# Hybrid mixer with expert retrieval on one core: another number of row steps for each stage of a front, an earlier first dot product, and a shorter pooling

## The chip, the cores and the metric

The kernel runs on one core of a Trainium2 chip. The metric is device time in microseconds (us). A difference of less than 0.3% (12 us) cannot be told from no change.

## The reference

One decoder layer over 1024 tokens of width 1024, in float32, batch 1, depth 1. Cut to what matters:

```python
proj = h @ w_in                       # pool values | z | x,B,C | dt | two gates
a    = pool_mixer(pool_in)            # 4 groups, trailing means of 2/4/8/16 tokens minus the token itself, per-group 256x256 map
m    = ssm_mixer(z, xbc, dt_raw)      # depthwise conv of 4 taps, SiLU, chunked scan (chunk 128), gate, grouped RMSNorm, @ ssm_out
h    = layer_norm(alpha * h + (sigmoid(g_pool) * a + sigmoid(g_ssm) * m) @ w_out)
# expert retrieval, 8 heads:
q = h @ w_q                           # per head two halves of 128
s = q . sub_keys                      # 128 scores per half; top 16 of each, 16 best sums of pairs -> 16 experts, softmax -> gate
hdot = sum_d h[t, d] * expert_u[idx[t, k], d]
out  = sum_k gelu(hdot[t, k]) * gate[t, k] * expert_v[idx[t, k], :]
h    = layer_norm(alpha * h + out)
```

Each token chooses 8 x 16 = 128 experts. For each it needs one row of 4 KB of `expert_u` and one of `expert_v`.

## The kernel before

**Two streams of work.** The tokens are cut into four superchunks of 256 (two tiles of 128). The *front* of a superchunk computes all that comes before the expert rows: projections, pooling, convolution, scan, merge, first layer norm, queries, top-k. The *rows* part gathers expert rows and uses them. A *pair* is one (tile, head, k): 128 tokens, one gather of 128 rows of `eu` for a dot product and one gather of 128 rows of `ev` for a weighted sum. There are 8 tiles x 128 = 1024 pairs.

**Steps.** Time is written by hand in steps: step p has the dot product of pair p on DVE (`dot`, L1401), and the weighted row of the pair 28 steps earlier (`LEAD`). That row is summed by DVE (`sum_row`, L1426) or by PE, as a matmul with a diagonal matrix (L549; 4 matmul records for a row), which ACT builds from the weights (L851, `vdiag`). The front of superchunk c is woven between the pairs of superchunk c-1: `until(p)` issues the pairs up to step p, `weave(p, front, n)` does so and lets n pieces of the front's DVE work in between, evenly spread. PE and ACT have programs of their own with the same step numbers, and meet DVE only at semaphores. ACT's GELU of a group of 16 pairs waits for its 16 dots, the weights of the group come two steps before its first row is due, and everything behind such a wait on ACT waits too.

**Stages of a front** (steps before: `STEPS` = 256 in all):

- A, four times (j = 0 to 3), 32 steps each: eight weight blocks of 1 MB on PE (L471, L479), pooling on DVE, convolution, transposes, then from offset 19 on the scan, in which PE, ACT and DVE take turns. DVE's pooling (`pooling`, L1144 to L1165) must end before PE's pool matmul (L580). From offset 20 DVE weaves the scan over the last 12 steps.
- Pair, four times 7 steps: gates and the output map of the scan. W, 16 steps: `w_out` and the layer norm.
- D0 and D1, 42 steps each: queries and scores on PE for four heads, then top-k, candidates and the choice of 16 experts on DVE (L1313 to L1383). D0 makes the indices of heads 0 to 3, D1 those of heads 4 to 7, in both tiles.

`EARLY` = 24: 24 dots come before superchunk 1's front, inside D1 of superchunk 0. The first front has no pairs beside it until then, and its last front ends at step 24 + 3 x 256 = 792. After step 800 (`PAIRED`) nothing is left but pairs, and u and v rows come in one gather of 8 KB rows (`euv`, L447); this stretch is called the tail.

**Who sums a row.** `share_of_pe(p)` gives PE a share of the rows due at step p; `assign_rows` adds the shares up and gives PE a row each time they reach 1, but never the first four and last three of a tile.

```python
    if off < ATC:
        return 0.4 if off % PA >= 19 else 0.0
    if off < ATW:
        return 0.0
    if off < ATD:
        return 0.4
    return 0.75
```

**Buffers and queues.** Single rows go through 12 buffers of 512 KB (`ROWS`), used in turn in the fixed order `ORDER`. POOL issues each gather (L432) once the pair of 12 places before has been used, and it waits for the indices of a half (`idx_ready`) only at that half's first dot. SP loads the weight blocks into a ring of four, each when PE has used its place. All these transfers share the core's 16 DMA engines.

Of the kernel before, what the change touches and what calls it, by code (L numbers as in the profile page):

```python
# [18 lines left out]
NC = SEQ // T  # L19
# [24 lines left out]
MAINS = AJ * MA + MC + MW + MD  # L44
TA, TW, TD = 12, 4, 8
TURNS = AJ * TA + TW + TD
# [8 lines left out]
EARLY = 24  # L55
STEPS = UNITS * TOPK
PAIRS = NC * STEPS
TILE = PH * TOPK
PA, PC, PW, PD = 32, 7, 16, 42
ATC = AJ * PA  # L60
ATW = ATC + 4 * PC
ATD = ATW + PW

# [7 lines left out]

def share_of_pe(p):
# [49 lines left out]
def build(nc, x, xt, wblocks, wdt, poolw, pscale, convw, convb, dtb, alog, dskip, normw,  # L122
          ln1g, ln1b, ln2g, ln2b, subkt, eu, ev, euv, out):
    with ExitStack() as ctx:
# [33 lines left out]
        pcoef = sb("pcoef", [P, 4, 4])  # L158
# [119 lines left out]
        DECAYS = (7, 8, 10, 11)  # L278
        TURNED = 10
        CONV = (0, 1, 3, 4)  # L280
# [22 lines left out]

        def turns(c, m):


            if c > 0:
                return c * TURNS - AJ * len(CONV) + m
            j = min(m // TA, AJ)
            return m - j * len(CONV) - (sum(n < m - j * TA for n in CONV) if j < AJ else 0)  # L310

        def emptied(eng, c, m):

            eng.wait_ge(main_free, c * MAINS + m + BANKS)

# [4 lines left out]
        def step(c, off):  # L320

            return EARLY + (c - 1) * STEPS + off

# [25 lines left out]
        def _(sp):  # L349
# [17 lines left out]
            def load_xt(c):  # L367
                sp.dma_start(xT[:, :, :], xt[:, :, ds(c * T, T)]).then_inc(xt_ready, 16)

            def superchunk(c):  # L370
# [12 lines left out]
                sp.dma_start(xres, x[ds(c * T, T), :].rearrange("(t p) d -> p t d", p=P)).then_inc(xres_ready, 16)  # L383
# [21 lines left out]
        def _(pool):  # L405
# [18 lines left out]
            for n, (table, q, _, _) in enumerate(ORDER):  # L424
                c, u, k = q // STEPS, q // TOPK % UNITS, q % TOPK
# [9 lines left out]
            for n, (q, _, _) in enumerate(BOTH):  # L435
                c, u, k = q // STEPS, q // TOPK % UNITS, q % TOPK
# [16 lines left out]
        def _(pe):  # L453
# [5 lines left out]
            def bank(c, m, n):  # L459
                pe.wait_ge(main_free, c * MAINS + m + n + 1)  # L460
                return main[n % 2]

            def turn_bank(c, m, n):
                pe.wait_ge(turn_free, turns(c, m + n) + 1)
                return turn[n % 2]

            def channels(dst_, w, src):

                for ct in range(2):
                    for k in range(KD):  # L470
                        last = pe.matmul(dst_[:, ct * T:(ct + 1) * T], w[:, k, ct * P:(ct + 1) * P], src[:, k, :],  # L471
# [3 lines left out]
            def tokens(dst_, w, src):  # L475

                for t in range(NT):
# [615 lines left out]
        def _(dve):  # L1093
# [180 lines left out]
            def front_w(c):  # L1274

                for t in range(NT):
# [24 lines left out]
                    if t == 1:  # L1301
                        dve.drain()
# [331 lines left out]
```

## Time and profile before

| | |
|---|---|
| median of 3 runs | 3923.23 us (3921.2 to 3933.7) |
| the profiled execution: its own time | 3919.56 us |
| the profiled execution: span of its instructions | 3917.5 us |
| busy: PE, DVE, ACT, POOL | 79%, 78%, 24%, 54% |
| bytes moved | 1334 MB, 340 GB/s in the mean |

The span is the time from the first to the last instruction; the own time is 2.1 us longer. Busy times are unions of an engine's instructions. A DMA share of 1.00 says that each of the 16 engines had a packet under way all the time, not that it moved the most bytes it can, so the rate beside it is to be read too. The granted clock is that of PE as a share of 2.4 GHz, and its lower level is 0.50 (1.2 GHz).

### The profile page before, as it was taken

The page shows a single profiled execution, that of the slowest core. Times are in us where ns is not written, and L with a number is a line of the kernel's source. Part 1 is how long each engine was busy: PE and PEld are TensorE (multiplying, and loading weights), DVE is VectorE, ACT ScalarE, POOL GpSimd, SP SyncE. Part 2 cuts the span into 40 slices and gives each one's busy share as a digit, 9 for nine tenths or more (in the row PEclk, how much of TensorE's full clock was granted, in tenths as well). Part 3 has the DMA queues.
Part 4 walks back from the last instruction along what each step waited for, and adds up shares of the span by engine and source line. Part 5 has one row for each costly group of instructions (what it writes and reads, how often), then busy time and mean ns, then how long its engine had stood idle before and what let it go on. Part 6 is the DMA issues. An engine that isn't in the chain of part 4 may idle for free. (4 is left out here: it accounts for less than half of the span.)

```text
span 3917.5 us, 39965 instructions
## 1 busy us (share of the span) xinstructions
PE 3098.7 (79%) x12052; PEld 2225.5 (57%) x12052; DVE 3043.0 (78%) x8003; ACT 923.6 (24%) x2201; POOL 2108.0 (54%) x1839
## 2 busy tenths in 40 slices
PE   8999963899987777999898767998887766565665
PEld 7888852677776445777676435776775432121221
DVE  4442289878887899888877999888877898677667
ACT  3332102244412112344312112343311111011101
POOL 0000014667766667676665677766665667555553
PEclk9999986899998898999998888999998887786877
DMA  4333347999999999999999999999999999999997
GB/s 160 108 113 126 143 155 250 337 375 395 399 397 402 326 376 366 383 394 399 399 380 397 346 366 375 377 395 368 385 375 397 328 335 356 422 422 421 422 422 327
DMA packets 306565, 1333.72 MB, mean 340 GB/s; under 512 B 34352, under 2 KB 38832, under 8 KB 249008
## 3 DMA queue, kind: packets, MB, share of 16 engines
q0 software_dynamic: 262656, 1073.86, 71.0%
q1 hardware_dynamic: 42400, 252.61, 16.4%
q10 hardware_dynamic: 1296, 4.72, 0.3%
q8 instruction: 97, 1.59, 0.2%
q14 instruction: 116, 0.95, 0.1%
HBM read 1326.85 MB, written 4.19 MB: 340 GB/s over the span
## 5 line engine op out<-in xcount | busy, mean ns | idle before, releaser
L432 POOL DMA_INDIRECT rowbuf<-eu,idx x800 | 902.2, 1128 | 1002.0 <-DVE idx L1382 535.9
L1401 DVE CUSTOM_DVE_ANT_0 rowbuf<-rowbuf,hb 128x1024 f32<-128x1024 f32 x884 | 1078.0, 1220 | 155.2 <-DMA rowbuf<-eu,idx 79.9
L432 POOL DMA_INDIRECT rowbuf<-ev,idx x800 | 918.6, 1148 | 485.6 <-PE vbank L549 231.6
L549 PE MATMUL vbank<-rowbuf,vdiag 128*128 128x512 f32 x1340 | 750.4, 703 | 354.5 <-ACT vdiag L851 237.9
L471 PE MATMUL main<-xT,ring 128*128 128x256 f32 x3584 | 795.8, 382 | 79.1 <-ACT mm L894 67.2
L471 PEld LDWEIGHTS main<-xT,ring 128*128 128x128 f32 x3584 | 688.5, 192 | 182.5 <-issue 87.9
L1426 DVE SCALAR_TENSOR_TENSOR acc<-rowbuf,hact,acc 128x1024 f32<-128x1024 f32 x549 | 705.1, 1284 | 101.9 <-DMA rowbuf<-ev,idx 93.7
L549 PEld LDWEIGHTS vbank<-rowbuf,vdiag 128*128 128x128 f32 x1340 | 281.4, 223 | 742.3 <-issue 409.6
L851 ACT ACTIVATE vdiag<-ident,hact 128x128 f32<-128x128 f32 x417 | 149.1, 393 | 468.1 <-DVE hact L1409 463.6
L654 PE MATMUL main<-late,ring 128*128 128x256 f32 x1024 | 233.0, 390 | 21.1 <-issue 15.3
L471 PE MATMUL main<-early,ring 128*128 128x256 f32 x1024 | 232.6, 387 | 0.7 <-ACT early L1014 0.7
L654 PEld LDWEIGHTS main<-late,ring 128*128 128x128 f32 x1024 | 199.4, 196 | 53.8 <-issue 18.7
L479 PE MATMUL main<-ring,xT 128*128 128x256 f32 x1024 | 226.2, 379 | 0.0
L471 PEld LDWEIGHTS main<-early,ring 128*128 128x128 f32 x1024 | 199.4, 195 | 40.8 <-issue 12.9
L479 PEld LDWEIGHTS main<-ring,xT 128*128 128x128 f32 x1024 | 194.5, 190 | 26.5
L1368 DVE SCALAR_TENSOR_TENSOR late<-iota,late,merged 128x50 f32<-128x50 f32 x1024 | 206.9, 266 | 0.8
L534 PE MATMUL turn<-craw_ln,cdiag 128*128 128x256 f32 x768 | 173.8, 378 | 0.0
L447 POOL DMA_INDIRECT rowbuf<-euv,idx x84 | 108.1, 1287 | 95.1 <-DVE acc L1426 77.6
L534 PEld LDWEIGHTS turn<-craw_ln,cdiag 128*128 128x128 f32 x768 | 145.3, 189 | 20.6
L669 PE MATMUL main<-ring,merged 128*128 128x256 f32 x512 | 119.0, 395 | 20.8 <-DVE merged L1271 20.8
L549 PE MATMUL vbank<-ring,vdiag 128*128 128x512 f32 x128 | 83.2, 797 | 60.1 <-ACT vdiag L851 60.1
L669 PEld LDWEIGHTS main<-ring,merged 128*128 128x128 f32 x512 | 101.5, 199 | 40.2 <-DVE merged L1271 22.4
(227 smaller groups left out, 3433.1 us busy)
## 6 DMA issues: line engine op xcount, KB each, us to landing
ring<-wblocks SPq DMA_DIRECT2D x224, 1024.0 KB, 8.1
rowbuf<-eu,idx POOLq DMA_INDIRECT x800, 8.5
rowbuf<-ev,idx POOLq DMA_INDIRECT x800, 8.4
xT<-xt SPq DMA_DIRECT2D x4, 1024.0 KB, 17.1
pw<-poolw SPq DMA_DIRECT2D x16, 256.0 KB, 8.2
zy<-x SPq DMA_DIRECT2D x4, 1024.0 KB, 12.7
h_out<-acc ACTq DMA_DIRECT2D x8, 512.0 KB, 7.8
craw_ln<-ln1g SPq DMA_DIRECT2D x4, 512.0 KB, 15.2
```

The source lines that it names most:

```text
L432: pool.indirect_dma_start(rows[r], None, (eu, ev)[table], bass.IndirectOffsetOnAxis(ap=idx[c % 2][:, u, k:k + 1], axis=0)).then_inc(row_re ...
L447: pool.indirect_dma_start(both[r], None, euv, bass.IndirectOffsetOnAxis(ap=idx[c % 2][:, u, k:k + 1], axis=0)).then_inc(both_ready[r], 16)
L471: last = pe.matmul(dst_[:, ct * T:(ct + 1) * T], w[:, k, ct * P:(ct + 1) * P], src[:, k, :], start=(k == 0), stop=(k == KD - 1))
L479: last = pe.matmul(dst_[:, t * 256:(t + 1) * 256], src[:, k, t * P:(t + 1) * P], w[:, k, :], start=(k == 0), stop=(k == KD - 1))
L534: last = pe.matmul(dst_[:, ct * T:(ct + 1) * T], cdiag[:, ct, k, :], craw[:, n % 2, ct, k:k + T], start=(k == 0), stop=(k == TAPS - 1))
L549: last = pe.matmul(vbank[half][:, :], vdiag[:, n % DIAGS, :], r[:, half * 512:(half + 1) * 512], start=first, stop=False, skip_group_check ...
L654: last = pe.matmul(dst_[:, ct * T:(ct + 1) * T], (lo, hi)[k // KD][:, k % KD, ct * P:(ct + 1) * P], yT[:, k, :], start=(k == 0), stop=(k = ...
L669: last = pe.matmul(dst_[:, n * 256:(n + 1) * 256], merged[:, k, t * P:(t + 1) * P], w[:, k, :], start=(k == 0), stop=(k == KD - 1))
L851: act.activation(vdiag[:, n % DIAGS, :], ident[:, :], ACT.Copy, scale=hact[:, g % 2, q % TOPK:q % TOPK + 1]).then_inc(vdiag_ready, 1)
L1368: dve.scalar_tensor_tensor(out=sel1[:, k, :], in0=iota[:, :], scalar=posf[:, u, k:k + 1], in1=candi[:, u, :], op0=ALU.is_equal, op1=ALU.mu ...
L1401: last = dve.tensor_tensor_reduce(r, r, hb[c % 2][:, t, :], 1.0, 0.0, ALU.mult, ALU.add, hdot[:, g % 2, k:k + 1])
L1426: dve.scalar_tensor_tensor(out=a, in0=r, scalar=hact[:, g % 2, k:k + 1], in1=a, op0=ALU.mult, op1=ALU.add).then_inc(row_free, 1)
```

## The change

- **Steps by stage.** `WIDTHS` gives the steps of A, pair, W, D0 and D1: 128, 28, 16, 42, 30 for superchunk 0 and 112, 28, 16, 52, 48 for the others (before: 128, 28, 16, 42, 42 for all). A front of a later superchunk still has 256 steps. All places within a stage are scaled to its new length and rounded down: `place(c, x)` gives a function from the old offset to the step. One j of A now has 28 steps, and its old offset 19 lies at 16, old 20 at 17, old 30 at 26.
- **First dots.** `EARLY` is 30: dot products begin with the first step of D1 of superchunk 0, where before 18 of its 42 steps went by first. The last front ends at step 798.
- **Shares.** PE's shares of rows are a table: 0.4 in the scan part of A, 0.4 in W, 0.75 up to step offset 30 of D (old offsets) and 1.0 after it, for superchunks 1 to 3. In the tail 0.6 as before.
- **Pooling.** Group j needs one window only. DVE now makes j+1 doublings instead of four, and one combining operation at the end instead of one after each (two for superchunk 0). The table of coefficients `pcoef` goes.
- **Bookkeeping.** Sizes, bank numbers and semaphore counts come from a list of tiles by superchunk (`CHUNK`), which is 2, 2, 2, 2, so that the numbers are the old ones. `scan_post` gets one more wait.

```diff
+CHUNK = (2, 2, 2, 2)
+NC = len(CHUNK)
-EARLY = 24
-STEPS = UNITS * TOPK
+WIDTHS = ((128, 28, 16, 42, 30),) + ((112, 28, 16, 52, 48),) * 3
+EARLY = 30
+BEGIN = [EARLY + sum(map(sum, WIDTHS[1:c])) - (0 if c else sum(WIDTHS[0])) for c in range(NC)]
+END = EARLY + sum(map(sum, WIDTHS[1:]))
+EDGES = (0, ATC, ATW, ATD, ATD + PD, ATD + 2 * PD)
+
+def step(c, off):
+    stage = max(n for n in range(5) if EDGES[n] <= max(off, 0))
+    length = EDGES[stage + 1] - EDGES[stage]
+    return BEGIN[c] + sum(WIDTHS[c][:stage]) + (off - EDGES[stage]) * WIDTHS[c][stage] // length
...
 def share_of_pe(p):
-    at, off = divmod(p - EARLY, STEPS)
-    if at == NC - 1:
+    if p >= END:
         return 0.6
+    c, off = position(p)
     if off < ATC:
-        return 0.4 if off % PA >= 19 else 0.0
+        return SHARES[c][0] if off % PA >= 19 else 0.0
     if off < ATW:
         return 0.0
     if off < ATD:
-        return 0.4
-    return 0.75
+        return SHARES[c][1]
+    return SHARES[c][2] if off < ATD + 30 else SHARES[c][3]
+
+SHARES = ((0.0, 0.0, 0.0, 1.0),) + ((0.4, 0.4, 0.75, 1.0),) * 3
...
+        def place(c, x):
+            return lambda off: step(c, x + off)
...
             def pooling(c, j, first):
                 dve.wait_ge(pool_raw, c * AJ + j + 1)
-                E = HALO + T
+                tc = CHUNK[c] * P
+                E = HALO + tc
                 src, dst_, reach = praw, psa, 1
-                for w in range(4):
+                for w in range(j + 1):
                     lo = 2 * reach - 1
                     dve.tensor_tensor(dst_[:, :, lo:E], src[:, :, lo:E], src[:, :, lo - reach:E - reach], ALU.add)
                     dve.drain()
...
+                    if w < j:
+                        src, dst_, reach = dst_, (psb if dst_ is psa else psa), 2 * reach
+                        yield
...
+                dve.scalar_tensor_tensor(out=pooled[:, :, start:tc], in0=dst_[:, :, HALO + start:E], scalar=1.0 / WINDOWS[j],
+                                         in1=praw[:, :, HALO + start:E], op0=ALU.mult, op1=ALU.subtract
+                                         ).then_inc(pool_done, 1)
...
                 y = yg[:, t, gg * GW:(gg + 1) * GW]
+                if s == 1:
+                    emptied(dve, c, j * MA + 10)
                 dve.tensor_tensor(y, yt1[:, :], zs[:, t, gg * GW:(gg + 1) * GW], ALU.mult)
...
             for c in range(NC):
                 for j in range(AJ):
-                    o = step(c, j * PA)
-                    until(o + 4)
+                    o = place(c, j * PA)
+                    until(o(4))
...
-                        weave(o + 12, pooling(c, j, False), 4)
-                    until(o + 16)
-                    weave(o + 18, merge_pool(c, j), 1)
-                    until(o + 20)
-                    weave(o + 32, scan(c, j), 18)
+                        weave(o(12), pooling(c, j, False), 4)
+                    until(o(16))
+                    weave(o(18), merge_pool(c, j), 1)
+                    until(o(20))
+                    weave(o(32), scan(c, j), 8 * CHUNK[c] + 2)
...
-                until(o + 5)
-                weave(o + PD, front_d(c, 0), 40)
-                weave(o + 2 * PD, front_d(c, 1), 40)
+                until(o(5))
+                weave(o(PD), front_d(c, 0), 18 * CHUNK[c] + 4)
+                weave(o(2 * PD), front_d(c, 1), 18 * CHUNK[c] + 4)
```

## Rows read from the trace of the kernel before

**Rows 1.** Page: span, busy times, and the DMA share in 40 equal slices.

```profile
span 3917.5 us, 39965 instructions
...
PE 3098.7 (79%) x12052; PEld 2225.5 (57%) x12052; DVE 3043.0 (78%) x8003; ACT 923.6 (24%) x2201; POOL 2108.0 (54%) x1839
...
DMA  4333347999999999999999999999999999999997
```

**Rows 2.** Stretches: length, busy PE, PEld, DVE, ACT, POOL, clock, DMA share, GB/s.

```profile
557.00:653.00 96.00, 28.80 (x126) 24.80 (x125) 88.53 (x530) 12.07 (x28) 33.80 (x35) 0.64 0.66 223
653.00:1087.00 434.00, 379.75 (x1732) 308.55 (x1730) 376.04 (x614) 160.92 (x394) 300.62 (x252) 0.93 0.97 374
1525.00:1957.00 432.00, 394.92 (x1814) 322.62 (x1813) 385.73 (x626) 171.08 (x418) 302.84 (x258) 0.96 1.00 394
1957.00:2120.00 163.00, 136.16 (x591) 111.75 (x592) 122.78 (x169) 25.04 (x44) 99.32 (x87) 0.91 0.98 389
2120.00:2269.00 149.00, 126.02 (x427) 79.76 (x426) 127.66 (x593) 27.98 (x63) 94.93 (x86) 0.89 0.96 363
2269.00:2399.00 130.00, 85.53 (x193) 39.86 (x192) 122.33 (x577) 14.29 (x39) 92.53 (x83) 0.84 0.96 352
2399.00:2842.00 443.00, 396.97 (x1814) 323.43 (x1813) 385.35 (x626) 170.87 (x417) 300.28 (x257) 0.95 0.98 383
2724.00:2842.00 118.00, 101.90 (x464) 83.11 (x464) 95.44 (x155) 43.32 (x106) 74.09 (x64) 0.92 0.93 356
3284.00:3899.00 615.00, 365.47 (x574) 128.94 (x575) 431.73 (x651) 65.73 (x206) 320.44 (x258) 0.77 1.00 415
```

**Rows 3.** L1401 alone (dots, two records each): DVE busy, clock, DMA share, rate.

```profile
557.00:653.00 96.00, 28.45 (x47) 0.64 0.66 223
557.00:683.00 126.00, 43.08 (x71) 0.67 0.74 255
1525.00:1957.00 432.00, 157.90 (x257) 0.96 1.00 394
2120.00:2399.00 279.00, 102.41 (x167) 0.87 0.96 358
```

**Rows 4.** L1426 alone (rows summed on DVE): the same columns.

```profile
1525.00:1957.00 432.00, 137.57 (x107) 0.96 1.00 394
2120.00:2399.00 279.00, 27.90 (x22) 0.87 0.96 358
```

**Rows 5.** L549 alone (rows on PE, four records each): PE, PEld, clock, DMA.

```profile
1525.00:1957.00 432.00, 42.12 (x80) 15.38 (x80) 0.96 1.00 394
2120.00:2269.00 149.00, 70.04 (x132) 27.19 (x132) 0.89 0.96 363
2269.00:2399.00 130.00, 73.21 (x124) 28.21 (x124) 0.84 0.96 352
```

**Rows 6.** All engines in short stretches of D and of one j.

```profile
2244.00:2268.00 24.00, 23.02 (x96) 16.55 (x95) 23.55 (x139) 3.92 (x9) 17.00 (x16) 1.00 1.02 409
2304.00:2328.00 24.00, 14.19 (x25) 5.41 (x24) 21.99 (x91) 3.95 (x10) 17.34 (x14) 0.86 0.91 316
1641.00:1699.00 58.00, 57.59 (x273) 50.48 (x271) 52.75 (x71) 25.14 (x68) 46.70 (x38) 1.00 1.02 405
1699.00:1745.00 46.00, 40.46 (x182) 30.03 (x183) 39.59 (x82) 15.93 (x36) 28.00 (x25) 0.93 1.00 382
```

**Rows 7.** PE's waits from 2700 to 2850: total, times, longest.

```profile
PE vbank L549 <- ACT vdiag L851: 18.9, 2, 9.9
```

**Rows 8.** PE's waits in A of superchunk 2: total, times, longest.

```profile
PE turn L580 <- issue: 7.0, 1, 7.0
```

**Rows 9.** PE's timeline in A of superchunk 1: start, length, idle before.

```profile
682.51 3.75 PE L580 MATMUL turn<-lexp,pw 128*128 128x256 f32 x8 [20.19 <-issue]
```

**Rows 10.** Page: DMA issues, us to landing.

```profile
rowbuf<-eu,idx POOLq DMA_INDIRECT x800, 8.5
```

**Rows 11.** Groups by line: pooling on DVE.

```profile
L1165 DVE SCALAR_TENSOR_TENSOR lexp<-scr,pcoef,lexp 128x512 f32<-128x512 f32 x36 | 27.0, 751 | 3.1 <-issue 0.4
```

More of the change, by code:

```diff
@@ L18 @@
 NT = T // P
-NC = SEQ // T
+CHUNK = (2, 2, 2, 2)
+NC = len(CHUNK)
+TILES = SEQ // P
+FIRST = [sum(CHUNK[:c]) for c in range(NC + 1)]
 WINDOWS = (2, 4, 8, 16)
@@ L485, in dt_product @@
                 pe.wait_ge(xt_ready, (c + 1) * 16)
-                pe.wait_ge(st_used, c * 4 * AJ + STATE)
-                for t in range(NT):
+                pe.wait_ge(st_used, scans(c, 0, 0) + STATE)
+                for t in range(CHUNK[c]):
                     for k in range(KD):
@@ L601, in front_a2 @@
                 dst_ = turn_bank(c, j * TA, 7)
-                for t in range(NT):
+                for t in range(nt):
                     for ct in range(2):
@@ L606, in front_a2 @@
                 last.then_inc(turn_ready, 1)
-                for t in range(NT):
+                for t in range(nt):
                     dst_ = turn_bank(c, j * TA, 8 + t)
@@ L698, in score @@
                     dst_ = turn_bank(c, AJ * TA + TW + i * 4, hh)
-                    for t in range(NT):
+                    for t in range(CHUNK[c]):
                         for side in range(2):
@@ L960, in front_a3 @@
             def front_a3(c, j):
-                o = step(c, j * PA)
-                for s in range(4):
-                    until(o + (20, 21, 23, 26)[s])
+                o = place(c, j * PA)
+                steps = 2 * CHUNK[c]
+                for s in range(steps):
+                    until(o((20, 21, 23, 26)[s]))
                     decays(c, j, s)
@@ L1257, in scan @@
                 yield from scan_pre(c, j, 0)
-                for s in range(4):
-                    if s < 3:
+                steps = 2 * CHUNK[c]
+                for s in range(steps):
+                    if s < steps - 1:
                         yield from scan_pre(c, j, s + 1)
@@ L1274, in front_w @@
             def front_w(c):
-                for t in range(NT):
+                for t in range(CHUNK[c]):
                     emptied(dve, c, AJ * MA + MC + 2 * t + 2)
@@ L1364, in choose @@
             def choose(c, i):
-                for u in range(8):
+                nt = CHUNK[c]
+                n_u = 4 * nt
+                for u in range(n_u):
                     for k in range(TOPK):
@@ L1539, in _ @@
                 for j in range(AJ):
-                    o = step(c, j * PA)
-                    until(o + 4)
+                    o = place(c, j * PA)
+                    until(o(4))
                     if c == 0:
-                        weave(o + 10, pooling(c, j, True), 4)
+                        weave(o(10), pooling(c, j, True), 4)
                         if j == 0:
```

538 lines of the change are left out of this document (290 added, 248 removed).

## The prediction

> **What bounds the kernel now.** I read the page first: two engines near 80% and a DMA share of nine tenths from the eighth slice on [rows 1]. Nothing is idle enough to name a bound, so I went to the table of stretches, cut where DVE starts a new stage [rows 2]. A superchunk's 256 steps are A, 432 us in superchunk 2; pair and W, 163; D0, 149; D1, 130. The tail is 615.
>
> - **A.** PE is busy 395 of 432 us, DVE 386, the DMA share is 1.00 at 394 GB/s [rows 2]. The short windows say which comes first. In the first part of one j (20 steps before the scan) PE works 57.6 of 58 us; in the scan part (12 steps) it works 40 of 46 and takes turns with DVE, 39.6 [rows 6]. So the first part lasts as long as PE's blocks, however few steps lie in it, and only the scan part can give way.
> - **D.** D1 has DVE busy 122 of 130 us, the rest being gaps of a fraction of a microsecond. PE is at 86. The DMA share of 0.96 looks full, but the rate is 352 GB/s. Windows of 24 us inside D show both cases: 409 GB/s at share 1.02, and 316 GB/s at 0.91 with DVE near its limit [rows 6]. I read it so: DVE bounds D1, and the transfers have about a tenth in hand.
> - **Tail.** Share 1.00, 415 GB/s [rows 2]: bound by transfers.
>
> Every step needs 2 x 0.524 = 1.049 MB. At 405 GB/s (between the best windows of A and D, [rows 6]) that is 2.59 us.
>
> **The change, part by part.**
>
> *D with 100 steps instead of 84.* Work of DVE now, D0 and D1: 250 us, of which dots 102.4 (84, so 1.22 each) and 27.9 for 22 rows summed (1.27 each) [rows 2 to 4]. That leaves 120, which I split as 61 in D0 and 59 in D1, like the busy times. New shares: I followed the planner's sum. PE gets 42 of 52 rows in D0 and 43 of 48 in D1 (31 and 32 of 42 before), which leaves DVE 10 and 5.
> D1: DVE 59 + 48 x 1.22 + 5 x 1.27 = 124, plus the 8 us of small gaps = 132. Transfers: 48 x 2.59 and 2 MB of others = 129. PE: 12 for its other work + 43 rows at 73.2/31 = 2.36 us = 114 [rows 5]. POOL: 92.5 us for 83 gathers, so 107 for 96, and gaps. I take 133.
> D0: DVE 61 + 52 x 1.22 + 10 x 1.27 = 137, plus the 21 us that it stands now = 158. Transfers: 52 x 2.59 + 10 MB of weights and others (25 us) = 160. PE: 56 + 42 x 70.0/33 = 145. The stands and the transfers overlap only in part now; I take 156.
> D = 289 instead of 279: +10 for 16 more steps. Lower bound: 280 (DVE's work and nothing else). Upper: 116.6 MB (99.8 now and 16 x 1.049) at D's own rate divided by its share, 358/0.96 = 373 GB/s [rows 3], is 313.
>
> *A with 112 steps instead of 128.* Transfers need 153.5 MB, 390 us at 394 GB/s. But PE's first part stays. In the scan part DVE loses 1.5 dots and about one summed row, 3 us. PE has 18 rows instead of 20, 2.1 us each [rows 5], inside this. So -3 us for each j, -12 for an A.
>
> *Pooling.* For superchunks 1 to 3 the four j need 10 doublings and 4 combinations instead of 16 and 16: 18 operations of about 0.75 us [rows 11], 13 us of DVE in an A. It lies in the first part, beside PE's blocks, so it costs and gives nothing, but for j = 0: there PE waits 7.0 us for the pooled values [rows 8], and they now come after one piece at the head of the weave instead of after the fourth. -6 in superchunks 2 and 3. If PE did not cover it, the 13 us would come off.
>
> *Late rows.* ACT builds no diagonal for steps behind old offset 30 of a j before DVE's sum of squares is done. By the planner's sum, PE has a row at offset 31 in four j: superchunk 1, j = 0; 2, j = 3; 3, j = 2 and 3. Two of them are the waits of 9 to 9.9 us of [rows 7]; the A of superchunk 3, 443 us instead of 432, has two. In the new plan the row behind that place (offset 27 of 28) comes once in each superchunk, in j = 2. One wait less, in superchunk 3: -9. What is queued behind such a wait is PE's next weight block, and behind it ACT's copies.
>
> *A together*: superchunk 1 -10 (it starts a little later, below), 2 -18, 3 -27: -55. D: 3 x 10 = +30. Pair and W have the same steps and work: 0.
>
> *First dots.* The gather's landing takes 8.5 us [rows 10], and with a dot in the first step DVE stands for it, where before 18 steps of top-k covered it. D1 of superchunk 0 then has DVE's 60 us of other work (88.5 - 28.5) [rows 2, 3], 30 dots (37 us) and two rows: it ends near 557 + 9 + 101 + some gaps = 670 with 30 dots, where before 24 were done at 653 [rows 3]. But the front of superchunk 1 starts at that step. Before, 35 dots were done at 683 [rows 3], when PE's wait of 20 us for the first pooled values ended [rows 9]. Now 34 or 35 are done at about 680, and the pooled values come there too. So dots from the first half on give 0 here (-3 to +5): they move six dots in and the front six steps back.
>
> *Tail.* It starts at step 798 instead of 792: six steps at 615/231 = 2.66 us, -16. Its price is in D, counted above.
>
> *At nothing.* The new wait in `scan_post` asks for a bank that the scan's earlier piece for step 2 has already waited for. Numbers by `CHUNK` are the old ones. Five small memsets go under the first load. PE's 59 more rows need ACT's diagonals: ACT is busy 42 of 279 us in D [rows 2].
>
> **Sum**: -55 + 30 + 0 - 16 = -41. From the profiled execution's 3919.6: 3878.6. The median of the runs shown is 3.7 us above it, so 3882; I say 3880.
>
> A page speaks against this; rival 1 works the same mechanism out from rows. The Trainium skill, "DMA: Bandwidth & Descriptors", section Specifications, puts what the HBM gives one core at about 358 GB/s. D runs at 352 to 363 GB/s [rows 2], as if it had met that limit; by that rule D would take 116.6/0.358 = 326 us, and the result would be 111 us above mine, 3991. The trace disagrees where it can: A has 394, the tail 415, and a window in D 409 [rows 2, 6].
>
> **Rivals.**
>
> 1. *D is full already; slower.* The mechanism is the share of 0.96: the gathers of single rows with few weight blocks beside them give no more than 373 GB/s. D takes 313 us, 24 more than I say, three times: 3880 + 72 = 3952. For it: a share of 0.96 in both halves of D. Against: DVE is at 94% in D1 with 42 steps, so a slow rate there is what DVE asks for. It decides from D = 303 on (3 x 14 = 41). Chance 0.12.
> 2. *A shrinks with its steps.* The bound of A is transfers and PE's full windows are a coincidence: A = 390, 23 less than I say, three times: 3811. For it: share 1.00. Against: 57.6 of 58 us. Chance 0.08.
> 3. *A new wait takes A's gain; no change.* With j of 28 steps, GELU groups of 16 fall on another place in each j (with 32 they fell on the same). If ACT then stands at a GELU when PE needs a bank, or PE's late rows get more, A keeps its length but for the pooling, and 35 to 40 us of the gain go: about 3917. For it: such waits cost more than themselves. The j of superchunk 3 that begins behind the first of [rows 7] takes 118 us at a clock of 0.92 [rows 2], where the one of [rows 6] takes 104. Chance 0.14.
>
> My own forecast has 0.66; its own range is 3850 to 3910.
>
> **The numbers.** Range: 3840 at the bottom (A a third of the way to rival 2, or D at 280), 3930 at the top (rival 3, and D at 303). It leaves out most of rivals 1 and 2. Faster by over 0.3% (below 3911): 0.63 of my own and rival 2, with a little of rival 3: 0.74. Within 0.3%: 0.14. Slower: 0.12.
>
> **What would show it.** D about 289 us with the rate at 400 GB/s and share 1.00, and DVE at 90% or more in D1: right; a rate below 380 with DVE at 85% is rival 1. A near 413 to 418 with its share below 1.00 and PE still without gaps in the first part: right; 390 to 400 is rival 2. PE's wait for L580 gone in superchunks 2 and 3. Waits of PE for a diagonal of 9 us at the end of j = 2 only; more of them, or in the middle of a j, is rival 3. The last front ends some 26 us earlier, at step 798 instead of 792, and a tail of about 599 us follows. The prediction is wrong if PE's rows in D0 hold back its queries, so that top-k starts late: D0 above 165 us.

## The result and the profile after

The changed kernel takes 3955.63 us (median of 6 runs, 3946.91 to 3959.93), the kernel before on the same chip 3928.75 (3921.2 to 3933.7). The ratio is 1.0068, with a 95% interval of [1.0053, 1.0084]: slower by 0.7%, where 3880 was forecast. The profiled execution took 3958.2 us against 3919.6 before.

The page of the changed kernel, its span, busy times and DMA share in 40 slices, to be held against [rows 1]:

```profile
span 3956.2 us, 40307 instructions
...
PE 3163.2 (80%) x12288; PEld 2245.8 (57%) x12288; DVE 2920.5 (74%) x7843; ACT 940.7 (24%) x2258; POOL 2096.1 (53%) x1839
...
DMA  4233346999899999999899999999899999999997
```

DVE has 122 us less to do, PE 64 more, and three slices that were 9 are now 8: the transfers have room, and the time is longer all the same.

The table of stretches of the changed kernel, cut at the same places of its stages as [rows 2] (same columns):

```profile
566.00:672.00 106.00, 13.14 (x48) 9.58 (x48) 98.80 (x542) 7.36 (x12) 40.78 (x39) 0.57 0.64 212
672.00:1088.00 416.00, 380.87 (x1763) 313.98 (x1762) 331.86 (x554) 161.97 (x404) 261.43 (x225) 0.95 0.94 359
1553.00:1982.00 429.00, 393.40 (x1795) 322.44 (x1796) 334.41 (x555) 165.58 (x408) 262.02 (x224) 0.94 0.93 355
1982.00:2145.00 163.00, 131.29 (x576) 108.53 (x575) 123.10 (x167) 27.36 (x46) 96.65 (x86) 0.91 1.00 393
2145.00:2303.00 158.00, 127.92 (x424) 77.14 (x422) 137.48 (x612) 28.38 (x68) 111.06 (x102) 0.96 1.00 384
2303.00:2449.00 146.00, 113.39 (x310) 54.64 (x308) 127.88 (x589) 22.60 (x60) 110.61 (x102) 0.98 1.00 383
2449.00:2873.00 424.00, 387.43 (x1795) 317.89 (x1796) 334.88 (x556) 165.57 (x408) 261.16 (x225) 0.95 0.94 360
3341.00:3938.00 597.00, 360.26 (x573) 127.77 (x572) 414.54 (x624) 64.08 (x204) 307.99 (x245) 0.79 1.00 417
1864.00:1982.00 118.00, 108.07 (x483) 87.75 (x484) 84.25 (x142) 41.88 (x105) 65.97 (x56) 0.92 0.85 321
```

Three things stand here beside [rows 2]. D1 takes 146 us where it took 130. A takes 416 to 429 us where it took 432 to 443, and in superchunks 2 and 3 it takes 429 and 424 where 414 and 416 were forecast. The last row is the fourth j of superchunk 2: 118 us, at a clock of 0.92.

The lengths below are differences between the ends of dot products, which mark the stages on DVE (SC is superchunk, and all stage lengths from here on are taken this way):

| us | SC 1 before, after | SC 2 before, after | SC 3 before, after |
|---|---|---|---|
| A, j = 0 | 100.4, 89.3 | 112.3, 102.7 | 112.5, 101.4 |
| A, j = 1 | 118.6, 105.6 | 106.7, 105.8 | 108.6, 105.4 |
| A, j = 2 | 107.0, 103.1 | 107.7, 102.8 | 104.7, 99.8 |
| A, j = 3 | 107.8, 117.6 | 105.1, 118.2 | 118.1, 117.5 |
| pair | 100.2, 104.0 | 104.4, 104.6 | 104.4, 103.5 |
| W | 58.1, 57.2 | 59.0, 58.1 | 58.3, 57.7 |
| D0 | 150.6, 158.1 | 148.3, 157.7 | 147.6, 157.8 |
| D1 | 129.2, 145.5 | 129.7, 146.5 | 130.9, 148.3 |

The last front ends at 3340.7 instead of 3284.2, and the rest of the span is 615.5 instead of 633.2. So the loss lies ahead of the tail: in D1, in the fourth j, and in the front of superchunk 1, which starts 19 us later (the table does not show that).

**D1.** POOL's waits in D1 of superchunk 2, in the kernel before (2269 to 2399): the line that waited, for what, total, times, longest.

```profile
POOL rowbuf L432 <- issue: 18.9, 62, 0.3
POOL rowbuf L432 <- DVE hdot L1401: 17.4, 17, 1.9
```

The same view of the changed kernel (2303 to 2449; its gathers are at L499):

```profile
POOL rowbuf L499 <- issue: 27.4, 90, 0.3
POOL rowbuf L499 <- PE vbank L619: 9.6, 12, 4.1
```

Before, POOL stood 17.4 us for DVE to give back a row buffer: DVE set the pace. In the changed kernel that wait is gone from the list. Ninety times POOL stands 0.30 us for nothing that the profile shows, and goes on with its next gather. Its timeline from 2323 (start, length, and in brackets the idle time before):

```profile
2323.28 0.93 POOL L499 DMA_INDIRECT rowbuf<-eu,idx  x1 [0.30 <-issue]
2324.52 0.94 POOL L499 DMA_INDIRECT rowbuf<-ev,idx  x1 [0.30 <-issue]
2325.76 0.94 POOL L499 DMA_INDIRECT rowbuf<-eu,idx  x1 [0.31 <-issue]
2327.00 1.79 POOL L499 DMA_INDIRECT rowbuf<-ev,idx  x1 [0.30 <-issue]
```

Since no other engine releases them and they are always 0.30 or 0.31 us, I count these pauses as the gathers' own. With them POOL is busy 111 + 27 = 138 of 146 us. The 9.6 us in which it waits until PE has used a row buffer (the line names `vbank`, the tile that PE's matmul writes) make up the rest of the stretch. A gather costs 1.08 + 0.30 us, and with the waits for PE the pace is 146/102 = 1.43 us each. Of the 102 gathers, 96 are for the 48 steps. The others were left over from D0: by a count of the gathers in the trace, POOL is 9 ahead of the steps where D0 begins and 5 where it ends, and it is back at 12 at the end of D1. In the kernel before it is 12 ahead at the end of D0.

**The fourth j.** PE's waits in A of superchunk 2 of the changed kernel (1553 to 1982), against [rows 8]:

```profile
PE ybank L587 <- issue: 17.4, 4, 6.2
PE vbank L619 <- ACT vdiag L927: 12.0, 3, 9.9
```

The 7 us for the pooled values are gone. The longest wait for a diagonal is there once. ACT's timeline and PE's, where the fourth j begins:

```profile
1863.44 0.20 ACT L1049 ACTIVATE rms<-rms 128x4 f32<-128x4 f32 x1 [16.47 <-DVE rms L1334]
...
1866.07 0.39 ACT L927 ACTIVATE vdiag<-ident,hact 128x128 f32<-128x128 f32 x1
```

```profile
1866.51 3.78 PE L619 MATMUL vbank<-rowbuf,vdiag 128*128 128x512 f32 x4 [9.88 <-ACT vdiag L927]
```

ACT stands 16.47 us for DVE's sum of squares, makes the diagonal behind it, and PE has waited 9.88 us for it. A window at that place (columns of [rows 2]) and DVE's waits in the whole j:

```profile
1855.00:1867.00 12.00, 2.12 (x7) 1.40 (x7) 11.48 (x23) 2.74 (x7) 7.91 (x6) 0.50 0.93 342
```

```profile
DVE scr L1289 <- ACT btok L1021: 13.4, 1, 13.4
```

The granted clock of these 12 us, in which PE works 2.12, is 0.50, the lower of the two levels, 1.2 GHz. Later in the same j DVE waits 13.4 us for ACT's `btok`, which ACT makes from PE's blocks. So a j with a wait of 9.9 us ahead of it takes 118 us, where the second j takes 106.

**The front of superchunk 1.** Its A ends at 1089.3 us, where it ended at 1088.8 before, although it has 16 steps fewer. PE's timeline of the kernel before, to be held against [rows 9], and then of the changed one, with the pooling's last operation on DVE:

```profile
632.76 15.74 PE L471 MATMUL main<-xT,ring 128*128 128x256 f32 x64 [67.20 <-ACT mm L894]
```

```profile
659.92 3.75 PE L619 MATMUL vbank<-rowbuf,vdiag 128*128 128x512 f32 x4 [92.86 <-DMA rowbuf<-ev,idx]
663.47 14.22 PE L539 MATMUL main<-xT,ring 128*128 128x256 f32 x64
...
681.52 0.69 DVE L1247 SCALAR_TENSOR_TENSOR lexp<-scr,mm 128x512 f32<-128x512 f32 x1
...
693.48 1.89 PE L651 MATMUL turn<-lexp,pw 128*128 128x256 f32 x8
```

DVE has the pooled values at 682 us, as the prediction said (about 680). But PE's pool matmul comes at 693.5 instead of 682.5, because PE is late with its weight blocks: it stands 92.9 us for one v row and starts the third and fourth block at 663.5, where it was at 632.8. By the planner's sum this is the row of pair 4, due at step 32. The share of 1.0 late in D of superchunk 0 now covers the steps 28 and 29, in which rows are already due. Those rows are among the first four of a tile and can't go to PE, so the sum stays full, and PE gets the first row that it may have. PE's program has this row between the second and the third block of the first j. In the kernel before PE's first row was that of pair 17.

### The profile page after: what moved, and what is told of

Same layout as the page of the kernel before. It is cut to its first block, busy times and chain, and to the rows that moved or that the text cites. A ratio compares the mean times of both kernels' runs of the same rounds, so it can differ in the third digit from the quotient of the medians.

```text
span 3956.2 us, 40307 instructions
## 1 busy us (share of the span) xinstructions
PE 3163.2 (80%) x12288; PEld 2245.8 (57%) x12288; DVE 2920.5 (74%) x7843; ACT 940.7 (24%) x2258; POOL 2096.1 (53%) x1839
## 4 chain that ended last, share of the span: by engine, by line
PE 44%; DMA 21%; DVE 16%; POOL 8%; issue 7%; DVEq 3%; ACT 2%; SPq 0%; ACTq 0%; POOLq 0%
PE main L539 18%; DMA rowbuf<-ev,idx 9%; PE vbank L619 6%; POOL rowbuf L499 6%; PE main L547 5%; DMA rowbuf<-euv,idx 4%; PE turn L604 4%; DVE rowbuf L1494 4%; DVE acc L1520 3%; PE main L742 3%; DMA ring<-euv,idx 3%; DMA merged<-euv,idx 2%; PE main L727 2%; DVE late L1460 2%; DMA rowbuf<-eu,idx 1%
## 5 line engine op out<-in xcount | busy, mean ns | idle before, releaser
L499 POOL DMA_INDIRECT rowbuf<-eu,idx x800 | 904.0, 1130 | 1041.8 <-DVE idx L1475 538.5
L499 POOL DMA_INDIRECT rowbuf<-ev,idx x800 | 905.1, 1131 | 498.1 <-PE vbank L619 237.4
L619 PE MATMUL vbank<-rowbuf,vdiag 128*128 128x512 f32 x1576 | 822.1, 659 | 407.2 <-DMA rowbuf<-ev,idx 257.6
L539 PE MATMUL main<-xT,ring 128*128 128x256 f32 x3584 | 799.3, 383 | 11.8 <-DMA ring<-wblocks 11.8
L619 PEld LDWEIGHTS vbank<-rowbuf,vdiag 128*128 128x128 f32 x1576 | 306.4, 208 | 843.2 <-issue 589.9
L539 PEld LDWEIGHTS main<-xT,ring 128*128 128x128 f32 x3584 | 691.0, 193 | 118.9 <-issue 23.3
L1520 DVE SCALAR_TENSOR_TENSOR acc<-rowbuf,hact,acc 128x1024 f32<-128x1024 f32 x490 | 629.9, 1285 | 113.8 <-DMA rowbuf<-ev,idx 105.6
L927 ACT ACTIVATE vdiag<-ident,hact 128x128 f32<-128x128 f32 x476 | 168.6, 393 | 454.0 <-DVE hact L1503 418.6
L539 PE MATMUL main<-early,ring 128*128 128x256 f32 x1024 | 231.9, 386 | 0.7 <-ACT early L1097 0.7
L539 PEld LDWEIGHTS main<-early,ring 128*128 128x128 f32 x1024 | 198.6, 194 | 40.2 <-issue 12.6
L604 PEld LDWEIGHTS turn<-craw_ln,cdiag 128*128 128x128 f32 x768 | 145.2, 189 | 22.8 <-ACT cdiag L882 2.3
```

Source lines behind the costliest of these rows:

```text
L499: pool.indirect_dma_start(rows[r], None, (eu, ev)[table], bass.IndirectOffsetOnAxis(ap=idx[c % 2][:, u, k:k + 1], axis=0)).then_inc(row_re ...
L539: last = pe.matmul(dst_[:, ct * tc:(ct + 1) * tc], w[:, k, ct * P:(ct + 1) * P], src[:, k, 0:tc], start=(k == 0), stop=(k == KD - 1))
L604: last = pe.matmul(dst_[:, ct * tc:(ct + 1) * tc], cdiag[:, ct, k, :], craw[:, n % 2, ct, k:k + tc], start=(k == 0), stop=(k == TAPS - 1))
L619: last = pe.matmul(vbank[half][:, :], vdiag[:, n % DIAGS, :], r[:, half * 512:(half + 1) * 512], start=first, stop=False, skip_group_check ...
L927: act.activation(vdiag[:, n % DIAGS, :], ident[:, :], ACT.Copy, scale=hact[:, g % 2, q % TOPK:q % TOPK + 1]).then_inc(vdiag_ready, 1)
L1520: dve.scalar_tensor_tensor(out=a, in0=r, scalar=hact[:, g % 2, k:k + 1], in1=a, op0=ALU.mult, op1=ALU.add).then_inc(row_free, 1)
```

## The experiments

All ratios are to the kernel before on the same chip, with their 95% intervals. The first four kernels ran on a chip on which the kernel before itself ranged from 3943 to 3983 us, so their intervals are wide. The change again, no late rows, old steps with no late rows, and short rows ran on a second chip, the other four on a third. Except for the second one, the excerpts compare each kernel with the changed one.

**Pooling alone.** Old steps, first dots and shares; what is left of the change is the shorter pooling and the bookkeeping.

```diff
-WIDTHS = ((128, 28, 16, 42, 30),) + ((112, 28, 16, 52, 48),) * 3
-EARLY = 30
+WIDTHS = ((128, 28, 16, 42, 42),) * 4
+EARLY = 24
-SHARES = ((0.0, 0.0, 0.0, 1.0),) + ((0.4, 0.4, 0.75, 1.0),) * 3
+SHARES = ((0.0, 0.0, 0.0, 1.0),) + ((0.4, 0.4, 0.75, 0.75),) * 3
```

> The changed kernel with the old steps (128, 28, 16, 42, 42 for all), the old first dot (24) and the old shares: what is left is the shorter pooling. Theory 1 (PE's blocks cover DVE's pooling, all but the wait for j = 0): A of superchunks 2 and 3 shorter by 6 to 10 us each, nothing elsewhere, 3905 to 3918 us. Rival (DVE's 13 us in each A come off in full, since the scan part gains too): 3875 to 3890.

Measured: 3947.43 us, 0.9967 [0.994, 0.9994]. The first j of superchunks 2 and 3 takes 108 and 107 us instead of 112; D1 stays at 129.5 to 131.3. But the whole A of superchunk 2 takes 435 us, where it took 432, and that of superchunk 3 440, where it took 444. So the pooling gives a little at most, and the 6 to 10 us in each A are not shown. With old steps and no late rows (below) the first j takes 111.5 and 112.3 us, as before.

**First dots alone.** The kernel above, with which the excerpt compares it, but with dots from the first step of superchunk 0's D1 on.

```diff
-WIDTHS = ((128, 28, 16, 42, 42),) * 4
-EARLY = 24
+WIDTHS = ((128, 28, 16, 42, 30),) + ((128, 28, 16, 42, 42),) * 3
+EARLY = 30
```

> The same, but with the first 30 dots in the second half of superchunk 0 (widths 128, 28, 16, 42, 30 there, first dot 30). Theory 1: the earlier dots buy nothing before step 34 (DVE stands 9 us for the first landing, the front starts later); the tail loses six steps, -16; the planner's late rows now end j = 0 in every superchunk, so that superchunk 2 gets a long j that it did not have, +11. Together within 10 us of the kernel with the pooling alone. Rival (the early gathers fill time in which the transfers were idle): 16 us or more below it.

Measured: 3986.16 us, 1.0074 [1.0044, 1.0103]: 39 us above the pooling alone, against an expectation of 10 at most. D1 takes 139 us, not 130, the second j of each A takes 118, and the A of superchunk 1 ends 24 us later (1118 instead of 1093.5). This is the first sign that six more steps in front shift something in all that follows. Which PE rows are late depends on the step number, and here the late ones stand after j = 0.

**Shares alone.** Pooling, old steps, and PE's shares as in the change.

```diff
-WIDTHS = ((128, 28, 16, 42, 30),) + ((112, 28, 16, 52, 48),) * 3
-EARLY = 30
+WIDTHS = ((128, 28, 16, 42, 42),) * 4
+EARLY = 24
```

> The kernel with the pooling alone and the new shares: PE gets every row in the later part of D, with the old steps. Theory 1 (in D the transfers carry about 384 GB/s at most, and DVE held them below that in the kernel before): D with 84 steps takes 99.8 MB / 384 = 260 us instead of 279, D1 about 118 to 122; two more late rows before a j of A cost 20; 3870 to 3895 us. Rival A (PE's rows in D are themselves the load, or give back their buffers late, and that is why D1 was 147 us in the changed kernel): D1 stays at 130 or above, 3910 or more.

Measured: 3960.25 us, 0.9978 [0.9948, 1.0009]. It says little. By the planner's sum the new shares make five late rows, four of them ahead of a j, and two j take 129 and 134 us. D1 takes 129 us where 118 to 122 were expected. But the trace also has slow places that no other engine explains. From 1905 to 1922 PE takes 17 us for 32 matmuls of its blocks, with pauses like this one, where a block of 32 takes 7.1 us elsewhere:

```profile
1913.14 1.10 PE L539 MATMUL main<-xT,ring 128*128 128x256 f32 x3 [0.63 <-issue]
```

From 2370 to 2382, in D1, DVE works 4.8 of 12 us, again without a releaser. Pauses of PE over 0.2 us between these matmuls (L539) stand in traces of this chip alone: 7.4 us in all in this run, 16.7 in the next, none in the traces of the change, of the kernel before and of the eight later runs. Another run, below, settles the point.

**Steps without shares.** The change, with 0.75 of the rows on PE in all of D.

```diff
-SHARES = ((0.0, 0.0, 0.0, 1.0),) + ((0.4, 0.4, 0.75, 1.0),) * 3
+SHARES = ((0.0, 0.0, 0.0, 1.0),) + ((0.4, 0.4, 0.75, 0.75),) * 3
```

> The changed kernel with the old share of 0.75 in all of D, and the new steps. Theory 1 (transfers bound D, DVE is close behind): D1 148 to 153 us as DVE has 13 rows more to sum, 3955 to 3975 us. Rival A (PE's rows hold D back): D1 falls below 140 us, 3940 or less.

Measured: 4044.64 us, 1.0192 [1.0149, 1.0235]. D takes 328, 323 and 316 us, and D1 of superchunk 2 has DVE at 140 of 152 us. The new steps don't go without the new shares: DVE would be the bound again, above POOL. The time is not D's alone: the fourth j take 133, 127 and 134 us, where the change has 118 with the same late rows, and all 16.7 us of PE's pauses lie in these three. Whether the pauses belong to the chip or to the kernels that ran on it is not shown.

**The change again,** unmodified, on the second chip, so that the next runs have it beside them.

> The changed kernel once more, beside the next three, since the chip of the first experiments scattered more than its own. 0.5 to 0.9% above the kernel before.

Measured: 3961.05 us, 1.0094 [1.0077, 1.0111]. D1 147, 150.5 and 149.7 us; fourth j 117 to 118.

**No late rows.** The change, but no row of A behind old offset 30 of a j goes to PE. DVE sums those rows.

```diff
-        return SHARES[c][0] if off % PA >= 19 else 0.0
+        return SHARES[c][0] if 30 > off % PA >= 19 else 0.0
```

> The changed kernel, where PE's share of rows is 0 from old offset 30 of each j on, so that PE never has a row whose diagonal waits for the sum of squares. Theory 2 (the late row of j = 2 costs the whole excess of j = 3, 118 us against 103): the fourth j of each A falls to 102 to 106 us, 35 to 45 us below the changed kernel. Rival (the fourth j is long because DVE has run ahead, or for transfers, and PE's wait is only where that shows): the wait goes elsewhere, less than 15 us.

Measured: 3926.96 us, 1.0012 [1.0002, 1.0022], 34 us below the change on the same chip, just under what was expected (35 to 45). The fourth j of superchunk 2 (columns of [rows 2]):

```profile
1855.00:1961.00 106.00, 99.55 (x463) 82.45 (x462) 85.07 (x143) 41.51 (x105) 65.25 (x57) 0.97 0.94 357
```

It takes 106 us instead of 118, at a clock of 0.97 instead of 0.92. Three late rows cost the change 34 us, 11 each. So the rival, that the wait only goes elsewhere, is out. D1 stays at 146 to 148 in this run, so it has a cause of its own.

**Old steps, no late rows.** Pooling alone with the same edit.

```diff
-WIDTHS = ((128, 28, 16, 42, 30),) + ((112, 28, 16, 52, 48),) * 3
-EARLY = 30
+WIDTHS = ((128, 28, 16, 42, 42),) * 4
+EARLY = 24
-        return SHARES[c][0] if off % PA >= 19 else 0.0
+        return SHARES[c][0] if 30 > off % PA >= 19 else 0.0
-SHARES = ((0.0, 0.0, 0.0, 1.0),) + ((0.4, 0.4, 0.75, 1.0),) * 3
+SHARES = ((0.0, 0.0, 0.0, 1.0),) + ((0.4, 0.4, 0.75, 0.75),) * 3
```

> The kernel with the pooling alone (old steps, old first dot, old shares) and no late rows. Theory 2: two of the four late rows stood before a further j of A and made it 117 us; both fall to 107, and the two before pair give little: 15 to 25 us below the kernel with the pooling alone, 0.8 to 1.0% below the kernel before. Rival: 0.3% as with the pooling alone.

Measured: 3875.76 us, 0.9875 [0.9859, 0.9892], a larger gain than was expected (0.990 to 0.992). From the second j on, all take 104 to 107 us. The step numbers of the kernel before had late rows as well [rows 7], and both kernels paid for them.

**Short rows.** The test of rival 1. The change, but in D1 of superchunks 1 to 3 every gather brings 768 of the 1024 columns, out of tables that hold only these. The last quarter of those dots and sums reads what the buffer held before. The number of gathers and of descriptors is the same, the bytes of D1's rows are three quarters.

```diff
+                at_ = q if table == 0 else step_of_v(q)
+                short = EARLY <= at_ < END and position(at_)[1] >= EDGES[4]
-                pool.indirect_dma_start(rows[r], None, (eu, ev)[table],
+                pool.indirect_dma_start(rows[r][:, 0:SHORT] if short else rows[r], None,
+                                        (eus, evs)[table] if short else (eu, ev)[table],
```

> The changed kernel, where the 96 gathers whose step lies in D1 of superchunks 1 to 3 bring 768 of a row's 1024 columns (the rest of the buffer keeps an older row, so that part of the products is made with old data). Same instructions on all engines, as many descriptors, a quarter fewer bytes. Theory 1 (transfers bound D1 in the changed kernel): D1 falls from 147 to 132 to 137 us, where DVE's 128 us and its gaps bound it. Rival B (POOL's issue, one gather each 1.4 us, bounds it): D1 stays within 3 us. Rival C (the stand is at the tile's edge alone, where seven rows and the layer norm fall on DVE): the first 42 steps keep their 121 us.

Measured: 3946.85 us, 1.0066 [1.0049, 1.0083]. D1 takes 143.6, 145.2 and 143.0 us, 3 to 7 less than in the change again, so neither the 132 to 137 of a D1 bound by transfers nor quite the 3 us at most of one bound by POOL. D1 of superchunk 2 with whole rows (the change again) and with short ones:

```profile
2295.00:2446.00 151.00, 111.78 (x308) 53.54 (x306) 129.26 (x594) 22.98 (x62) 116.27 (x102) 0.98 0.98 372
```

```profile
2295.00:2440.00 145.00, 113.02 (x309) 54.16 (x307) 127.83 (x592) 22.39 (x60) 110.62 (x101) 0.97 0.89 297
```

And POOL's waits in the latter:

```profile
POOL rowbuf L502 <- issue: 29.2, 96, 0.3
POOL rowbuf L502 <- PE vbank L623: 7.0, 5, 3.9
```

At 297 GB/s instead of 372 the stretch lasts 145 us instead of 151, and POOL still goes from gather to gather, at 110.62/101 = 1.10 us and 0.30. Had the bytes been the bound, the 56 MB of the one stretch would have become 43, and these take 116 us at 372 GB/s. So rival 1's mechanism is refuted. That its time, 3952, came nearly true is chance.

**Plain rows.** The change, but the 48 rows of v of each D1 come by a plain load of 512 KB on POOL's queue, from fixed places. The sums are then over other rows than the queries chose.

```diff
+                at_ = step_of_v(q)
+                if table == 1 and EARLY <= at_ < END and position(at_)[1] >= EDGES[4]:
+                    pool.dma_start(rows[r], ev[ds(n % 8 * P, P), :]).then_inc(row_ready[r], 16)
+                    continue
```

> The changed kernel, where the 48 v rows due in D1 of superchunks 1 to 3 come by a plain load of 128 consecutive rows on POOL's queue instead of a gather (wrong rows, so the weighted sum of those pairs is left out in effect). Same bytes, same work on DVE, PE and ACT. Theory 3 (the first experiments leave POOL's issue as D1's bound: 100 of 102 gathers there follow each other with the least gap, 1.09 and 0.36 us each, and a quarter fewer bytes took only 5 us off): if a plain load takes POOL less than 1.1 us, D1 falls to 136 to 142 us. Rival (transfers): D1 stays at 146 to 150. If a plain load takes POOL as long, nothing moves and it tells nothing.

Measured: 3938.1 us, 1.0035 [1.0022, 1.0049]. D1 takes 141.8, 142.0 and 141.4 us, as expected if POOL is the bound. D1 of superchunk 2, POOL's waits there, and its timeline:

```profile
2290.00:2432.00 142.00, 111.98 (x311) 54.20 (x309) 127.75 (x592) 22.49 (x60) 104.92 (x103) 0.99 1.02 406
```

```profile
POOL rowbuf L503 <- DVE hdot L1498: 15.8, 12, 2.7
POOL rowbuf L503 <- issue: 13.3, 44, 0.3
```

```profile
2321.26 0.59 POOL L501 DMA_DIRECT2D rowbuf<-ev  x1
2322.15 1.95 POOL L503 DMA_INDIRECT rowbuf<-eu,idx  x1 [0.30 <-issue]
```

With half of the gathers gone POOL waits for DVE again, 15.8 us, and the rate rises to 406 GB/s. That is the other side of the short rows: the transfers can do more than D1 asked of them. The pause of 0.30 us stands ahead of the gather and not ahead of the load. The gain is small for two reasons. The gathers alone (L503) take 78.09/57 = 1.37 us each here, not 1.08:

```profile
2290.00:2432.00 142.00, 78.09 (x57) 0.99 1.02 406
```

And DVE, at 128 of 142 us, is close behind. With its small gaps, 8 us in the kernel before, DVE alone would take some 136 us for this D1, which is an estimate. By it POOL's pace costs about 10 of the 146 us.

**The change with the old first dots and no late rows.**

```diff
-WIDTHS = ((128, 28, 16, 42, 30),) + ((112, 28, 16, 52, 48),) * 3
-EARLY = 30
+WIDTHS = ((128, 28, 16, 42, 42),) + ((112, 28, 16, 52, 48),) * 3
+EARLY = 24
-        return SHARES[c][0] if off % PA >= 19 else 0.0
+        return SHARES[c][0] if 30 > off % PA >= 19 else 0.0
```

> The changed kernel without late rows and with the old first dot (24, and 42 steps for D1 of superchunk 0), beside the same with 30 on the chip before (ratio 1.0012). Theory 4 (with 30, every tile's edge falls into the last six steps of D1, where DVE is full, 25 us for six steps; with 24 it falls into the first part of A, beside PE's blocks): D1 falls from 147 to 138 us, A stays, the tail has six steps more (+16): together -10 to -15, ratio 0.996 to 0.999. Rival (it is the number of steps alone): D1 stays within 3 us, ratio 1.004 or more.

Measured: 3910.78 us, 0.9956 [0.9939, 0.9972], where 0.996 to 0.999 was expected. Its D1 takes 142 to 144 us, where 138 were expected, against 146 to 148 with the first dots early. That is 12 us for the three. The larger part lies in superchunk 1. PE starts the third block at 637.3 us, and its pool matmul comes at 666.9 where the change has 693.5:

```profile
666.91 1.89 PE L651 MATMUL turn<-lexp,pw 128*128 128x256 f32 x8
```

The A of superchunk 1 ends at 1057 us, and at 1081 with the first dots early, both without late rows: 24 us. The tail gives 26 us of it back to the early dots.

**Old steps and no late rows, with the first dots early.**

```diff
-WIDTHS = ((128, 28, 16, 42, 30),) + ((112, 28, 16, 52, 48),) * 3
+WIDTHS = ((128, 28, 16, 42, 30),) + ((128, 28, 16, 42, 42),) * 3
-        return SHARES[c][0] if off % PA >= 19 else 0.0
+        return SHARES[c][0] if 30 > off % PA >= 19 else 0.0
-SHARES = ((0.0, 0.0, 0.0, 1.0),) + ((0.4, 0.4, 0.75, 1.0),) * 3
+SHARES = ((0.0, 0.0, 0.0, 1.0),) + ((0.4, 0.4, 0.75, 0.75),) * 3
```

> The best so far with the first 30 dots in the second half of superchunk 0. Theory 4: D1 of superchunks 1 to 3 rises from 130 to 139 us since it takes the tile's edge, A0 does not fall as much, the tail loses 16 us: ratio 0.989 to 0.993. Rival (the earlier start is a gain): below 0.986.

Measured: 3913.77 us, 0.9968 [0.9954, 0.9983], where 0.989 to 0.993 was expected. The first dots cost 38 us here against the run on the second chip, though no late row is left. D1 of superchunk 2 with first dots at the old place (old steps, no late rows) and at the new one:

```profile
2246.00:2376.00 130.00, 91.57 (x213) 44.32 (x212) 122.42 (x578) 15.56 (x43) 91.65 (x84) 0.83 0.96 357
```

```profile
2280.00:2418.00 138.00, 89.85 (x216) 44.21 (x214) 130.31 (x586) 14.28 (x35) 93.60 (x85) 0.81 0.95 357
```

DVE has 8 us more work within a D1 of the same 42 steps. Each front now begins six steps later in the order of the steps, so the edge of a tile (the last rows, which DVE sums, and the layer norm) lies six steps earlier within the front. This work leaves the first part of j = 0, where PE's blocks cover it, and comes to lie in the last steps of D1, where DVE is the bound. That is 27 us in the three D1 (8 to 9.5 each). The A of superchunk 1 ends 26 us later (1101 instead of 1075), with PE at its third block at 665.3 instead of 639.3, and the tail is 17 us shorter. The fourth j take 110 to 112 us here and 106 to 107 there, because a superchunk has two tile edges: the layer norm of its first tile, which came after A (at 1957.9 us in superchunk 2, whose A ended at 1940.8), now comes inside the fourth j (at 1975.3, before its end at 1976.7). The first j of superchunks 2 and 3 give back 2.5 and 4 us.

**Old steps, no late rows, new shares.**

```diff
-WIDTHS = ((128, 28, 16, 42, 30),) + ((112, 28, 16, 52, 48),) * 3
-EARLY = 30
+WIDTHS = ((128, 28, 16, 42, 42),) * 4
+EARLY = 24
-        return SHARES[c][0] if off % PA >= 19 else 0.0
+        return SHARES[c][0] if 30 > off % PA >= 19 else 0.0
```

> The best so far (old steps, old first dot, shorter pooling, no late rows, ratio 0.9875) with the new shares, PE taking every row late in D. Theory 3: DVE bounded D1 with 42 steps, POOL's issue is next at 84 x 1.45 = 122 us, D1 falls from 130 to 122 to 127 and D0 by 0 to 3: ratio 0.980 to 0.987. Rival: no change, since POOL's issue and PE's rows take over at once.

Measured: 3847.92 us, 0.9797 [0.978, 0.9813]: faster than both kernels, 2.0% below the one before. D0 and D1 of superchunk 2, and POOL's waits in D1:

```profile
2086.00:2230.00 144.00, 120.50 (x406) 75.40 (x405) 121.72 (x588) 26.77 (x61) 90.83 (x83) 0.93 0.96 359
2230.00:2348.00 118.00, 92.13 (x234) 39.56 (x233) 110.37 (x567) 18.37 (x52) 89.91 (x83) 1.00 0.99 382
```

```profile
POOL rowbuf L499 <- issue: 21.3, 70, 0.3
POOL rowbuf L499 <- PE vbank L619: 11.1, 13, 4.4
```

D1 with 42 steps takes 118 us for 83 gathers, 1.42 each: the pace of POOL, as with 48 steps. So the new shares move D1's bound from DVE (130 us) to POOL (118), and each further step costs two gathers, 2.9 us by this pace.

## Why the prediction was wrong

The gap in the profiled executions is 3958.2 - 3878.6 = 80 us. Against the forecast D came out 47 us too long, A with the later start of superchunk 1 counted in 33, pair and W 1, and the tail 2 too short. By the steps of the prediction:

- **D1, the step that failed: "POOL: 92.5 us for 83 gathers, so 107 for 96, and gaps. I take 133."** D1 took 146 to 148 us, 14 more than said, three times: +41. The term was POOL's busy time, with its gaps left without a number. By the list of waits above these were 18.9 us before. With them the same row gives (92.5 + 18.9)/83 = 1.34 us a gather and 129 us for 96. That much stood in the trace of before and was not read. By itself it would still not have been the bound, beside DVE's 132. What the trace of before could not show is the rest: POOL leaves D0 with gathers to make up, so that it issues 102 in the stretch, and it waits for row buffers until PE has used them, now that PE has 43 of the 48 rows. That makes 1.43 to 1.48 us each and 146 to 151 us.
- **"So dots from the first half on give 0 here (-3 to +5)" failed twice.** The dots themselves came as said: 30 at 672 us (670 said), and the pooled values at 682 (680 said). But the front was held up: PE's pool matmul came 11 us later than before, behind the wait of 92.9 us for a v row that the new share of 1.0 had given to PE ahead of its weight blocks. Without late rows, early dots let the A of superchunk 1 end 24 us later (1081 instead of 1057); in the changed kernel it ended 10 us after its forecast. No run takes this one row alone away, so its part of the 24 is not shown. And the second tile edge of each superchunk moved into D1. With the new steps that is 12 of the 41 us above, with the old ones 27.
- **Late rows: "One wait less, in superchunk 3: -9."** The count was right, the price was not. One late row stands in each superchunk, in j = 2. Of the old ones, one in superchunk 2 and one in 3 stood ahead of pair, where they cost some 3 us (pair takes 104.4 twice, and 101.9 and 101.5 with old steps and no late rows). Now every one stands ahead of a j, and costs 11 to 13 us. In superchunk 2 the fourth j rose from 105.1 to 118.2, and in superchunk 3 it stayed (118.1 and 117.5), where -9 was forecast. That makes 22 of the 23 us by which these two A are too long. It was rival 3's mechanism in part, but through old waits at new places.
- **The step of A was right.** Against the old steps and shares, both without late rows, the new ones take 12 and 15 us off the A of superchunks 2 and 3 (430 and 431 become 418 and 416), where 12 were said; the first part does not shrink with its steps, and rival 2 is out. PE's wait of 7 us for the pooled values is gone, but the 6 us that this should give are not seen in the first j of that run with the old steps. In superchunk 1 it looks right for another reason. Without late rows its A ends at 1081, where 1079 was forecast, because errors cancel: the late row behind j = 0 gave 14 us when it went and the steps 18 (1075 becomes 1057), and the first dots took 24.
- **D0: 158 us** (156 said). **Tail: -17.7** (-16 said). Pair and W: within 4 us.
- **The transfers are not the bound of D1.** D ran at 383 to 384 GB/s here, above rival 1's 373. By the Trainium skill, "DMA: Bandwidth & Descriptors", section Specifications, about 358 GB/s would be the most that one core gets from the HBM. The traces disagree: A before ran at 374 to 394 GB/s and the tail at 415 [rows 2], and D here at 383 to 384. The short rows show that D1 does not wait for bytes.

With each run's ratio put on 3925 us, the change comes apart like this: pooling and no late rows -49, new shares -31, new steps +62, first dots early +22, late rows back in +32; together +37. The ratios come from two chips, and each of these terms is good to 8 or 9 us by their intervals. The steps are the surprise. Against the old steps with all else equal, superchunks 2 and 3 gain some 16 and 22 us in A (435 and 438 become 418 and 416) and lose 40 and 39 in D (262 and 263 become 302). A step costs an A, where PE's blocks cover it, about 1.2 us, and a D, where POOL has nothing to hide behind, 2.5. The change moved 16 of them from the one to the other.

What stays open: why about a third of the gathers in D1 take 1.15 to 1.9 us on POOL instead of 0.94, with rows of 3 KB as with rows of 4 KB; how much of the later start of superchunk 1 is PE's one early row; and what slows PE and DVE in the traces of the shares alone and of the steps without shares.

## What to carry to other kernels

Count a queue's own gaps as its work: "issue" waits of a constant 0.30 us beside each instruction make POOL's 92.5 of 130 us into 111, and a stage that is given more gathers comes close to that bound. Before moving steps between stages, price a step in each stage by what bounds it there, for every engine that has work in it and not only for the two busiest. A late instruction has no price of its own: a wait of the same kind cost 3 us ahead of one stage and 12 us ahead of another, so when numbers of steps shift, follow each late one to its new place, and each tile edge too. And look for the first instruction that a new share gives to an engine: one row too early on PE stood 92.9 us ahead of the blocks of a whole front.

## What the runs showed of the hardware

A gather of 128 rows held POOL 0.93 us at the least, with 0.30 us to the next, and 1.08 to 1.14 and 0.30 on the mean in D1; with rows of 3 KB instead of 4 KB it was no less (1.10). A plain load of 512 KB held it 0.59 us, and the gathers between such loads took 1.37 us on the mean. One core moved 417 GB/s in the tail, and 406 in a D1 with half of the gathers replaced, where 372 went with a DMA share of 0.98. So a share close to 1 did not mean that the transfers could do no more, and when the rows of D1 were cut to three quarters, at 297 GB/s, the share was still 0.89. PE's granted clock was 0.50 in the 12 us in which it worked 2.12, and 0.97 over the same j without the late row.
